# Attention's first loads, the output projection's weights and the first queries, issued at the end of the row tiles' program

## What is computed

```
h = modulate(rmsnorm(x, pre_mix_g), sh1, sc1)
q, k, v, z = in_proj(h, w_in)                    # 1024 -> 4 x 512
q = rope(q, pos); k = rope(k, pos)
o = attend(q, k, v, lam)                         # 4 heads, two softmaxes each, p[0] - lam * p[1]
o = rmsnorm(o, subln_g) * (1 - lam_init)
pz, pool_state = pool(z)
m = concatenate([o, pz]) @ w_out                 # 1024 x 1024
x = x + g1 * rmsnorm(m, post_mix_g)
h2 = modulate(rmsnorm(x, pre_ffn_g), sh2, sc2)
x = x + g2 * rmsnorm(moe_ffn(h2), post_ffn_g)    # 64 experts, top 8, and a shared one
```

## Time and profile before

| | |
|---|---|
| three timed runs | 1859.15, 1864.81, 1867.13 us; median 1864.81 |
| the profiled execution | 1860.37 us, its span 1858.6 us |
| mean granted TensorE clock | 0.959 |
| row tiles' program | to about 371 us |
| attention's program | from 371.4 us |
| experts' program | from about 852 us |

### The profile page before, as it was taken

How to read it: one execution, slowest core, us unless ns; L and a number is a source line. 1 busy time by engine, 2 the same in 40 slices (tenths; PEclk the granted TensorE clock), 3 DMA queues, 4 the chain that set the end, 5 groups by cost and what they waited for, 6 DMA issues and landing times.

```text
span 1858.6 us, 25684 instructions
## 1 busy us (share of the span) xinstructions
PE 1681.7 (90%) x8499; PEld 1211.4 (65%) x8500; DVE 1133.5 (61%) x1511; ACT 888.1 (48%) x1325; POOL 656.4 (35%) x555
## 2 busy tenths in 40 slices
PE   4978999679898998785999999999999999999995
PEld 3534555333346666453888888888888888888842
DVE  2235566552235456663777777777777777777627
ACT  1000111042236555223666666666666666666623
POOL 0044566500000000103455555555555555555300
PEclk9989999979999999787999999999999999999998
DMA  9567867578782112744898899899999989889736
GB/s 341 191 194 229 290 215 225 157 265 245 229 267 80 65 51 97 297 172 184 263 310 302 289 309 310 289 307 312 291 306 317 294 303 318 297 299 315 240 128 249
DMA packets 151909, 457.38 MB, mean 246 GB/s; under 512 B 29592, under 2 KB 39794, under 8 KB 126169
## 3 DMA queue, kind: packets, MB, share of 16 engines
q1 hardware_dynamic: 118377, 382.76, 56.7%
q0 software_dynamic: 30720, 69.83, 16.3%
q10 hardware_dynamic: 2680, 3.15, 0.5%
HBM read 403.40 MB, written 86.54 MB: 264 GB/s over the span
## 4 chain that ended last, share of the span: by engine, by line
PE 50%; DVE 1%; DMA 1%; issue 1%; ACT 0%; POOL 0%; SPq 0%; ACTq 0%; POOLq 0%; DVEq 0%
PE ps L2227 28%; PE ps L2244 14%; PE ps L2213 5%; PE ps L2526 1%; PE ps L2251 1%; PE ps L2544 1%; DMA a<-acc_d 1%; DMA xg<-h_d,tokb 0%; DVE a L2594 0%; DVE lo_gu L2272 0%; DVE a L2597 0%; DVE a L2582 0%; DVE xT_lo L2276 0%; DVE lo_dn L2272 0%; POOL xg L2136 0%
## 5 line engine op out<-in xcount | busy, mean ns | idle before, releaser
L2227 PE MATMUL ps<-hi_gu,xT_hi 128*128 128x512 f32 x768 | 309.1, 402 | 0.0
L2272 DVE TENSOR_TENSOR lo_gu<-raw_gu,hi_gu 128x1024 fp32r<-128x1024 f32 x256 | 304.1, 1219 | 4.5
L2227 PE MATMUL ps<-hi_gu,xT_lo 128*128 128x512 f32 x768 | 300.6, 391 | 0.0
L2227 PE MATMUL ps<-lo_gu,xT_hi 128*128 128x512 f32 x768 | 298.9, 389 | 0.0
L2166 ACT ACTIVATE hi_gu<-raw_gu 128x1024 fp32r<-128x1024 f32 x256 | 260.8, 1065 | 0.0
L2130 POOL DMA_INDIRECT acc_d<-yb,tokb x96 | 227.9, 2374 | 43.3 <-ACT yb L2180 28.3
L447 POOL TENSOR_TENSOR prod<-kring,qbc 128x512 f32<-128x512 f32 x128 | 160.6, 1288 | 203.5 <-DMA kring<-in_cache_k 148.3
L2111 POOL DMA_INDIRECT xg<-h_d,tokb x96 | 101.8, 1060 | 368.0 <-PE ps L2213 366.8
L600 PE MATMUL ps<-w_in_sb,hT 128*128 128x512 f32 x512 | 225.9, 599 | 1.1 <-ACT hT L467 1.1
L600 PEld LDWEIGHTS ps<-w_in_sb,hT 128*128 128x128 f32 x512 | 96.8, 192 | 119.3 <-issue 117.8
L2180 ACT ACTIVATE yb<-ps,wslot 128x1024 f32<-128x1024 f32 x96 | 107.0, 1115 | 137.4 <-PE ps L2244 137.4
(11 more groups left out here) (339 smaller groups left out, 2619.9 us busy)
## 6 DMA issues: line engine op xcount, KB each, us to landing
raw_gu<-in_expert_w_gate SPq DMA_DIRECT2D x64, 1024.0 KB, 8.2
raw_gu<-in_expert_w_up SPq DMA_DIRECT2D x64, 1024.0 KB, 11.7
raw_dn<-in_expert_w_down SPq DMA_DIRECT2D x64, 1024.0 KB, 7.1
kring<-in_cache_k SPq DMA_DIRECT2D x128, 256.0 KB, 3.3
vring<-in_cache_v SPq DMA_DIRECT2D x128, 256.0 KB, 3.0
adaw<-in_ada_w SPq DMA_DIRECT2D x12, 2048.0 KB, 10.6
w_in_sb<-in_w_in SPq DMA_DIRECT2D x4, 2048.0 KB, 20.0
a<-acc_d SPq DMA_DIRECT2D x16, 512.0 KB, 5.2
```

Source lines behind the costliest of these rows:

```text
L2227: last = pe.matmul(ps[:, 2 + b % 2, :].rearrange("p (a f) -> p a f", a=2), x[b % 2][:, k, :], w[:, :, k * F:(k + 1) * F], start=(k == 0 an ...
L2272: dve.tensor_tensor(lo_cut(n, u), raw_cut(n, u), hi_cut(n, u).bitcast(F32), ALU.subtract).then_inc(lo_made, 1)
```

## The change

SyncE issues w_raw's two halves and q_h(0) and q_h(1) at the end of the row tiles' program, behind the store of the pool state and ahead of the closing waits. The weights come first; between them and the queries SyncE waits until all eight stores to qT_d have landed. The four issues are taken out of attention's program, which now begins with load_pooled(0). The semaphores w_here and attn_q_in are made once, ahead of the row tiles' program, and kept over the clearing. The tiles q_h and w_raw are placed at the same addresses as before.

```
@@ the row tiles' tiles and semaphores @@
+        dead = at["cos"][0] * 4 / 1024
+        q_h = [place(f"q_h{j}", dead + 4 + 2 * j, [P, NH, P]) for j in range(2)]
+        w_raw = place("w_raw", 139, [P, KC, D])
+        w_here = [sem(f"w_here{j}", keep=True) for j in range(2)]
+        attn_q_in = [sem(f"attn_q_in{j}", keep=True) for j in range(2)]
+        wv = w_out[0].rearrange("(c p) n -> p c n", p=P)
@@ the end of SyncE's list in the row tiles' program @@
                 sp.dma_start(pool_prompt[0, 0], zb[0][P - BUF:P, :]).then_inc(misc_out, 16)
+                for j in range(2):
+                    sp.dma_start(w_raw[:, 4 * j:4 * j + 4, :], wv[:, 4 * j:4 * j + 4, :]).then_inc(w_here[j], 16)
+                sp.wait_ge(qT_out, 16 * NT)
+                for i in range(2):
+                    sp.dma_start(q_h[i][:, :, :], qT_d[:, :, i * P:(i + 1) * P].rearrange("h p t -> p h t")
+                                 ).then_inc(attn_q_in[i], 16)
                 for s_, v in ((k_out, 16 * (NT + 1)), (mods_rest_in, 16), (qT_out, 16 * NT), (mix_out, 16 * (NT + 1)),
                               (misc_out, 64), (sc_new_in, 16 * NS)):
                     sp.wait_ge(s_, v)
@@ attention: placements and semaphores @@
-        dead = at["cos"][0] * 4 / 1024
-        q_h = [place(f"q_h{j}", dead + 4 + 2 * j, [P, NH, P]) for j in range(2)]
-        w_raw = place("w_raw", 139, [P, KC, D])
-        w_here = [sem(f"w_here{j}") for j in range(2)]
-        q_in = [sem(f"attn_q_in{j}") for j in range(2)]
@@ attention: the beginning of SyncE's list @@
-                load_q(0)
-                wv = w_out[0].rearrange("(c p) n -> p c n", p=P)
-                for j in range(2):
-                    sp.dma_start(w_raw[:, 4 * j:4 * j + 4, :], wv[:, 4 * j:4 * j + 4, :]).then_inc(w_here[j], 16)
-                load_q(1)
                 load_pooled(0)
                 load_x(0)
@@ load_q and scores: the semaphore's name @@
-                                 ).then_inc(q_in[i % 2], 16)
+                                 ).then_inc(attn_q_in[i % 2], 16)
-                        pe.wait_ge(q_in[i % 2], 16 * (i // 2) + 16)
+                        pe.wait_ge(attn_q_in[i % 2], 16 * (i // 2) + 16)
```

## The result

The changed kernel's median is 1871.29 us (17 runs, 1869.17 to 1876.24) against 1864.81 before (17 runs, 1854.86 to 1868.73). The ratio is 1.005, 95% interval 1.0038 to 1.0061, which is 7.1 to 11.4 us on 1865. The two medians themselves are 6.5 us apart, just under that interval. The change made the kernel slower. The interval holds the bound of 0.5% (9.3 us), so whether the loss passes it stays undecided, and no part of it leaves room for a gain.

The account below looks back on a forecast made before the run. TensorE was busy 1681.7 of 1858.6 us in a chain of steps, with q_h(0) the only load on the path at the seam. 1862.6 plus 7.5 for the later q_h(0), other terms 0, gave 1870.1 us; range 1860 to 1878.

Parts of the forecast that it names:

- Weights moved up: At the seam, w_raw is issued 3.4 us earlier; worth nothing, since nobody waited for the weights.
- q_h moved behind the weights: At the seam, q_h(0) gets 4.2 MB ahead of it and lands at 381.7, starting the path 7.5 us later.
- upper bound +8.3: For q_h(0) behind the weights: landing at 382.5, if it takes the full 13.0 us of q_h(1) before.
- the 0.8 us that I took off: In q_h(0)'s landing estimate, 0.8 us subtracted because q_h(0) itself no longer stands ahead of the weights.
- The like row: The profile's row for q_h(1) before, issued 1.1 us behind the first weight issue and landing after 13.0 us.
- The drain: At the closing barrier behind the new issues: 0.2 us later, or attention opens at 374.5 on a stall; cost 0.
- That cover is gone if q_h(0) lands early.: At attention's first scores: a late barrier costs 0 only while GpSimd's reduction is done before a late q_h(0) lands.
- Does it reach the end: From attention's start to the kernel's end: a chain of steps, so the whole 7.5 us stays.
- Rival 1: At the seam, q_h(0) overtakes the weights and lands at 372.4, gaining 1.8 us: 1860.8 us; chance 0.06.
- Rival 2: In attention's value-page stream, a later start finds pages ready, repaying up to all 7.5 us: 1862.6 to 1870.1; chance 0.11.
- Rival 3: In attention, TensorE's clock rises later against the work: total over 9.3 us, up to +12.4 or 1875.0; chance 0.15.
- factor of 1.7: TensorE's work cost at the lower clock: four score matmuls of 256 columns took 1.23 us against 0.70.

Follow-up runs that it names:

- weights alone: Against the kernel before, only w_raw's halves issued at the end of the row tiles' program, both q_h loads left in attention's: 1872.0 us, ratio 1.0044.
- q_h(0) alone: Against the kernel before, only q_h(0) issued at the end of the row tiles' program, weights and q_h(1) left in attention's: 1862.99 us, ratio 0.9998.
- half ahead: Against the kernel before, the row tiles' program ends by issuing first weight half, q_h(0), second half, q_h(1): 1870.11 us, ratio 1.0035.
- all early swapped: Against the kernel before, all four loads early, q_h(0) first; attention's step 0 rounds w_raw before the decode scores' subtraction and exponential: 1863.27 us, ratio 0.9997.
- ScalarE's queue: Against the kernel before, weights early on SyncE; attention's program begins with q_h(0) issued by ScalarE and q_h(1) by SyncE: 1870.96 us, ratio 1.005.
- order alone: Against the kernel before, nothing issued early; attention's program begins with both weight halves, then q_h(0), then q_h(1): 1874.07 us, ratio 1.006.
- queries first: Against the kernel before, all four loads at the end of the row tiles' program: q_h(0), both weight halves, q_h(1): 1864.79 us, ratio 1.0015.
- half early swapped: Against the kernel before, q_h(0) and first weight half early; attention's step 0 rounds w_raw before the decode scores' subtraction and exponential: 1862.25 us, ratio 0.9992.

## Why the prediction was right

The time, 1871.29 us, lies 1.2 from the 1870.1 of the forecast, with the mechanism that it named. That the two are so close is partly luck: the forecast started from 1862.6, and the median of the kernel before came out 2.2 higher; by the medians the delay is 6.5 in place of 7.5, by the ratio 9.3, by the traces 8.1. By its own steps:

- *Weights moved up: worth 0.* Right. The first rounding again has no wait before it.
- *q_h moved behind the weights: +7.5, upper bound +8.3.* It was +8.1. The term that was mis-sized is the 0.8 us that I took off for q_h(0)'s own share of the queue. q_h(0) needed 12.9 us from its issue, like q_h(1) of before with its 13.0; the weights' landings came down only by 0.3 and 0.1 us (7.8 and 12.6 for 8.1 and 12.7). The like row itself, with nothing taken off, would have been the better value. (The landing of q_h(0) before was 371.39 + 2.9 = 374.3 and not 374.2, so the prediction's own numbers give +7.4 and +8.2.)
- *The drain: barrier later by 0.2, or opening at 374.5 if the issue stalls; cost 0 either way.* The stall came: 3.2 us, opening at 374.03 in the new trace, which is 374.9 by the clock of the one before. It cost 0, as the weights alone show, whose barrier is at its old place and whose loss is the same. One premise was wrong: the reduction was not done when q_h(0) landed. It started at 383.28, 1.8 us after the landing, since it came 9.2 us behind the opening and not 6.4; it still ended 2.8 us before VectorE's subtraction at 386.59.
- *"That cover is gone if q_h(0) lands early."* Right, and larger than the words suggest. GpSimd's reduction turned out to be the next bound, close behind: with q_h(0) in front it takes back 2.9 us of 2.9.
- *Does it reach the end: whole.* Right within the intervals of the table.
- *Rival 1 (q_h(0) not held up, gain 1.8 us)* did not happen, and its price was wrong too. I let the gain pass to the end unhindered, although the step on the drain had named the reduction. The kernel with q_h(0) alone in front has that early landing and gains nothing.
- *Rival 2 (repaid by the value pages)* fell. The wait for those pages was 49.0 us in 50 places, 47.8 in 47 before. I misread that row: it adds the waits of the weight loads (36.9 us before) to those of the matmuls, which overlap. The matmuls alone waited 10.9 us before and 10.9 with the change, and no more than that could have been repaid.
- *Rival 3 (clock)* fell in the form that it was given, a later rise against the work. The first rise came at about 404.0, 22.5 us behind the first score matmul, where it was 23.1 before (397.4 - 374.3). These rows and the next are us, TensorE busy, granted clock, DMA share, GB/s:
```profile
403.00:404.00 1.00, 1.00 (x10) 0.50 0.00 0
404.00:405.00 1.00, 0.61 (x8) 0.98 0.00 0
```
  But the profiled execution has a dip later on that the one of before has not:
```profile
433.00:434.00 1.00, 0.41 (x1) 1.00 0.96 340
434.00:435.00 1.00, 0.31 (x1) 0.88 0.77 248
435.00:436.00 1.00, 1.00 (x2) 0.50 0.82 262
...
438.00:439.00 1.00, 1.00 (x6) 0.91 0.80 244
```
  TensorE had stood idle for 0.6 and 1.3 us for value pages just ahead of it, then worked at 1.2 GHz for 3.4 us. At the same place before, it stood idle for 0.6 and 1.1 us, and the clock stayed at 1.00. From the first eviction of the decode sums to the second it took 23.9 us (418.79 to 442.67) where before it took 21.1 (411.98 to 433.05). That is 2.8 us, of which the lower clock explains some 1.4 by the prediction's factor of 1.7 (an estimate); the rest was not followed up. This profile's span is 10.4 us longer: 8.1 at the start and 3.0 in the rest, less the 0.85 us by which the store to mix_d was early.

  The last two columns of the table show that such things come and go, and that the rest goes with the clock. The three executions with 50 to 53 us at 1.2 GHz have 455.8 to 456.2 us, the seven with 56 to 69 have 458.7 to 461.9. The first rise came 0.6 to 2.2 us behind the first value matmul in seven of the ten, and 6.6 to 7.3 us behind it in the other three (weights alone, half ahead, all early swapped). Neither follows the delay: the kernel on ScalarE's queue, 8 us late at the start, has 455.9, and the one that starts earliest has 461.9. So rival 3 priced something real, but it is a scatter between executions: over the timed runs of the kernel before, the mean granted clock goes from 0.952 to 0.961. The profile of before was one with little time at the lower clock, which fits its total, 4.4 us under the median.

The doubt whether the loss passes 0.5% was real: the interval of the ratio reaches to both sides of that bound.

## What to carry to other kernels

Before a load is moved up, ask two things: who waits for it, and what will now stand behind it. Here the load moved to the front had 1.7 us to spare and the one that went behind it had none, and 4 MB at 400 GB/s is 10 us of delay for whoever comes next, behind a barrier or not. Issue small loads that start the chain first, and do not count on another queue to save them: in the one kernel that tried it, with short packets against long ones, it gained nothing. If the first wait is removed, look up the second: a gain is worth only the distance to the next late comer, and work that has its data can be put into that gap.

## What the runs showed of the hardware that was not expected

- **GpSimd's first reduction over partitions starts late by an amount that varies with what is in flight.** From the opening of the program to its start: 6.4 us before, 9.2 with the change, 9.3 with the weights alone, 7.9 with the order alone, 7.7 with q_h(0) alone, 11.1 with the queries first, 8.7 with half ahead, 10.5 on ScalarE's queue, 10.0 with all early swapped and 9.6 with half early swapped. It is 6.4 to 7.9 where the weights are issued after the opening and 8.7 to 11.1 where at least half of them was in flight at it. The queue holds two instructions at line 1065 that set GpSimd's configuration, for which no transfer is shown. The Trainium skill, page "GPSIMD Engine Reference", section "Terminology", says that such an instruction brings a library of GpSimd's code in by DMA at run time. That would fit; no run here isolates it, and why it took 11.1 us with the queries first and 9.3 with the weights alone stays open.
- **Two queues shared by packets, not by bytes**: 171 packets of 512 bytes against 169 of 4 KB in 2 us, so 0.09 MB against 0.69; in the next 2 us 172 against 176.
- **The time at the lower TensorE clock differs between the ten profiled executions by up to 19 us in the same stretch** (50 to 69 us of 456 to 462), and the stretch is up to 6 us longer with it. No run isolates which of the two brings the other about. Two kernels are better compared by distances close to the change than by the spans of two single profiles.
- **The issue of a load can stall**: the fourth load at the seam took 0.51 us before and with the queries first, 3.2 with the change, 3.1 with the order alone and 3.6 with half ahead. What decides it was not tried.
